# Last two feed-forwards multiply high and low input parts as one 512-column operand; recurrent gates take their Exp before their Ln

## The reference

```
def swiglu_2(u, w1, w3, w2):
    return (jax.nn.silu(u @ w1) * (u @ w3)) @ w2
```

## Time and profile before

| | |
|---|---|
| median of 3 runs | 2218.63 us (2211.37 to 2218.75) |
| profiled execution | 2217.61 us, of which the span is 2215.8 us |
| busy share of the span | TensorE 96%, its weight loads 86%, VectorE 72%, ScalarE 43% |
| L514, matmuls of all up steps | 7392, 903.3 us busy |
| L529, matmuls of the down steps | 1512, 355.0 us busy |
| L752, low parts of weights | 224, 512.5 us busy |
| L712, modulation rows (two groups) | 240, 294.3 us busy |
| granted TensorE clock, mean | 0.98 of full speed |

### The profile page before, as it was taken

The page is one execution under the profiler, slowest core; times in us unless marked ns, Lnnn a source line. Parts: engine busy times, 40 slices in busy tenths (PEclk is TensorE's granted clock), DMA queues, the critical chain, the costliest instruction groups (busy, mean ns, idle before and its releaser), DMA issues. The chain is left out here.

```text
span 2215.8 us, 37819 instructions
## 1 busy us (share of the span) xinstructions
PE 2125.2 (96%) x16108; PEld 1901.7 (86%) x16108; DVE 1596.1 (72%) x2307; ACT 959.2 (43%) x1330; POOL 2.3 (0%) x8
## 2 busy tenths in 40 slices
PE   7999999999999999999999899999899999999998
PEld 5999899887899999977999689888699996759997
DVE  4887877766787888766887678486677776666545
ACT  3444534426544353435434476343453444225333
POOL 0000000000000000000000000000000000000000
PEclk7999999999999999999999899999999999999999
DMA  9866588440688778733987112400278822305551
GB/s 395 329 245 259 219 318 337 156 153 3 231 353 322 292 285 322 312 143 121 368 322 299 46 58 83 154 15 3 79 278 349 346 91 84 152 1 198 196 185 38
DMA packets 65814, 450.86 MB, mean 203 GB/s; under 512 B 7959, under 2 KB 9240, under 8 KB 12696
## 3 DMA queue, kind: packets, MB, share of 16 engines
q1 hardware_dynamic: 65688, 449.11, 52.6%
HBM read 448.03 MB, written 1.05 MB: 203 GB/s over the span
## 5 line engine op out<-in xcount | busy, mean ns | idle before, releaser
L514 PEld LDWEIGHTS banks<-ffn_h_split,ffn_weights_split 128*128 128x128 f32 x7392 | 898.8, 192 | 13.3 <-DVE ffn_weights_split L589 4.7
L514 PE MATMUL banks<-ffn_h_split,ffn_weights_split 128*128 128x256 f32 x7392 | 903.3, 284 | 6.6 <-DVE ffn_h_split L610 6.3
L752 DVE TENSOR_TENSOR ffn_weights_split<-weight_ring,ffn_weights_split 128x2048 fp32r<-128x2048 f32 x224 | 512.5, 2288 | 236.8 <-ACT ffn_weights_split L656 236.8
L656 ACT CAST ffn_weights_split<-weight_ring 128x2048 fp32r<-128x2048 f32 x224 | 426.2, 1903 | 172.7 <-PE banks L529 165.0
L529 PE MATMUL banks<-ffn_weights_split,ffn_hidden_split 128*128 128x512 f32 x1512 | 355.0, 390 | 1.8 <-DVE ffn_hidden_split L689 1.8
L529 PEld LDWEIGHTS banks<-ffn_weights_split,ffn_hidden_split 128*128 128x128 f32 x1512 | 279.8, 188 | 57.6 <-DVE ffn_hidden_split L689 2.2
L624 ACT ACTIVATE ffn_arena<-banks 128x256 f32<-128x256 f32 x154 | 59.1, 384 | 504.5 <-PE banks L514 504.5
L712 DVE CUSTOM_DVE_ANT_0 weight_ring<-weight_ring,first_arena,cols 128x1024 f32<-128x1024 f32 x200 | 245.3, 1279 | 0.4 <-ACT first_arena L666 0.4
L696 DVE TENSOR_TENSOR ffn_arena<-banks,ffn_arena 128x256 f32<-128x256 f32 x154 | 64.8, 421 | 46.5 <-ACT ffn_arena L624 46.4
L539 PE MATMUL banks<-ffn_weights_split,ffn_hidden_split 128*128 128x512 f32 x336 | 77.6, 390 | 0.0
L539 PEld LDWEIGHTS banks<-ffn_weights_split,ffn_hidden_split 128*128 128x128 f32 x336 | 62.6, 188 | 12.7
(11 more groups left out here) (399 smaller groups left out, 2486.7 us busy)
## 6 DMA issues: line engine op xcount, KB each, us to landing
weight_ring<-in_weights SPq DMA_DIRECT2D x407, 1024.0 KB, 4.9
first_arena<-in_norm_rows SPq DMA_DIRECT2D x12, 512.0 KB, 7.1
first_arena<-in_c_rows SPq DMA_DIRECT2D x4, 512.0 KB, 11.6
first_arena<-in_ctx_rows SPq DMA_DIRECT2D x2, 1024.0 KB
h<-in_ctx SPq DMA_DIRECT2D x1, 1024.0 KB, 17.6
side<-in_x SPq DMA_DIRECT2D x1, 1024.0 KB
x<-in_x_rows SPq DMA_DIRECT2D x1, 1024.0 KB
hyena_tables<-in_hy_filt SPq DMA_DIRECT2D x1, 1024.0 KB
```

What stands on the lines that cost most here:

```text
L514: last = nc.tensor.matmul(bank[:, half * T:half * T + T], w[:, x, sl], hs[:, k, y, :], start=(k == 0 and x + y == 0), stop=(k == DT - 1 an ...
L656: nc.scalar.copy(wsplit[:, c % S, 0, :], raw).then_inc(self.split_hi.sem, 1)
L752: nc.vector.tensor_tensor(wsplit[:, c % S, 1, :], core.wbuf[:, (self.first + at(c)) % NSLOT, :], wsplit[:, c % S, 0, :].bitcast(F32), ALU. ...
```

## The change

In feed-forwards A and B (`wide=True`) the high and low parts of the input, which lie side by side, are the one moving operand of a 512-column matmul with the high weights; the product with the low weights stays a matmul of 256 columns, added onto the first half. A half of a tile now fills a whole bank, so a tile takes two banks and the four banks hold two tiles. The two 256-column halves of a bank must be added: ScalarE copies the second halves of both banks to SBUF (`copy_low`), VectorE adds the first halves to them (`add`), and only then follow Silu and the gate product. The order of the steps in the loop over c is changed too: copy, hidden_hi, Silu, weights on ScalarE; add, hidden_lo, gate, weights on VectorE.

In the recurrent stage the four Exp come first and the four Ln together after them; an evacuation of PSUM lies between. The high and low parts of chunk lv0 are made before the gates' loop instead of after it, and those of lv1 move up to about where lv0's were.

```diff
+        def up_wide(p, par, c, place, r=0, opening=False):
+            for t in range(2):
...
+                if not (opening and p == 0):
+                    pe.wait_ge(self.summed.sem, p * 2 + (self.summed.base + t - 1))
+                w = wsplit[:, (c + t) % S, :, :]
+                for half in range(2):
+                    bank = core.ps[4 + 2 * t + half]
+                    for k in range(DT):
...
+                        nc.tensor.matmul(bank[:, :], w[:, 0, sl], hs[:, k, :, :].rearrange("p y t -> p (y t)"),
+                                         start=(k == 0), stop=(k == DT - 1), skip_group_check=True)
+                        last = nc.tensor.matmul(bank[:, 0:T], w[:, 1, sl], hs[:, k, 0, :], start=False, stop=(k == DT - 1),
+                                                skip_group_check=True)
+                last.then_inc(self.multiplied.sem, 1)
...
+        def copy_low(q):
+            act.wait_ge(multiplied.sem, multiplied.base + chunk_of_tile(q) + 1)
+            if q >= 2:
+                act.wait_ge(self.gated.sem, self.gated.base + q - 1)
+            at = 4 + 2 * (q % 2)
+            nc.scalar.copy(f["sums"][:, q % 2, :, :], core.banks[:, at:at + 2, T:2 * T]).then_inc(self.copied.sem, 1)
+
         def silu(q):
...
+            if self.wide:
+                act.wait_ge(self.summed.sem, self.summed.base + q + 1)
+                raw = f["sums"][:, q % 2, 1, :]
...
         for c in range(1, 3 * PAIRS):
             q = TILE_OF.get(c - S)
+            if q is not None and self.wide:
+                copy_low(q)
+            if waiting is not None and self.wide:
+                hidden_hi(waiting)
             if q is not None:
                 silu(q)
-            if waiting is not None:
+            if waiting is not None and not self.wide:
                 hidden_hi(waiting)
...
+        def add(q):
+            dve.wait_ge(self.copied.sem, self.copied.base + q + 1)
+            at = 4 + 2 * (q % 2)
+            nc.vector.tensor_tensor(f["sums"][:, q % 2, :, :], core.banks[:, at:at + 2, 0:T], f["sums"][:, q % 2, :, :],
+                                    ALU.add).then_inc(self.summed.sem, 1)
...
             q = TILE_OF.get(c - S)
+            if q is not None and self.wide:
+                add(q)
+            if waiting is not None and self.wide:
+                hidden_lo(waiting)
             if q is not None:
                 gate(q)
...
             step(nc.scalar.activation(b["ea"][:, :], b["a_log"][:, :], ACT.Exp))
+            high("lv0")
             for i in range(4):
                 act.wait_ge(steps.sem, steps.base + 6 + 3 * i + 2)
                 step(nc.scalar.activation(lt[:, i, :], lt[:, i, :], ACT.Exp))
-                step(nc.scalar.activation(lt[:, i, :], lt[:, i, :], ACT.Ln, bias=core.one[:, 0:1]))
             act.wait_ge(padded.sem, padded.base + 1)
             half_out("gk00", raw_pair(0, 0))
+            for i in range(4):
+                step(nc.scalar.activation(lt[:, i, :], lt[:, i, :], ACT.Ln, bias=core.one[:, 0:1]))
             last_out("gk01", "gk0", raw_pair(0, 1))
-            high("lv0")
+            high("lv1")
...
-            high("lv1")
...
+            low("lv0")
             for i in range(4):
-                dve.wait_ge(exps.sem, exps.base + 3 + 2 * (i + 1))
+                dve.wait_ge(exps.sem, exps.base + 7 + i + 1)
...
-            low("lv0")
+            low("lv1")
             products(0), products(1)
...
-            low("lv1")
```

More of the change, by code:

```diff
@@ L457, in __init__ @@
     def __init__(self, core, h, f, tail, sides=None, refresh=None, modulate=None, vector=None, before=None,
-                 opening=None, split_next=False, ahead=()):
-        self.opening, self.split_next, self.ahead = opening, split_next, ahead
+                 opening=None, split_next=False, ahead=(), wide=False):
+        self.wide, self.opening, self.split_next, self.ahead = wide, opening, split_next, ahead
         self.core, self.h, self.f, self.tail, self.sides, self.refresh = core, h, f, tail, sides, refresh
@@ L469, in __init__ @@
         self.hid_hi, self.hid_ready = take("ffn_hidden_hi", FFT), take("ffn_hidden_ready", FFT)
+        self.copied, self.summed = take("attn_exp", FFT if wide else 0), take("attn_p_ready", FFT if wide else 0)
         self.modulated = take("ffn_modulated", DT + 1 if modulate else 0)
@@ L492, in pe @@
         assert all(at(c + 6 * r) == at(c) + body * r for c in range(5, 11) for r in range(rounds))
+        def up_wide(p, par, c, place, r=0, opening=False):
+            for t in range(2):
+                if opening and p == 0 and t == 0:
+                    pe.wait_ge(self.first_lo.sem, self.first_lo.base + 1)
+                else:
+                    pe.wait_ge(used.sem, r * body + (first + place[t] + 1))
+                if not (opening and p == 0):
[4 more added lines that the diff above has]
+                    for k in range(DT):
+                        if opening and p == 0 and t == 0 and half == 0:
+                            pe.wait_ge(self.h_lo.sem, self.h_lo.base + max(k, 1) + 1)
+                        sl = slice(k * 2 * P + half * P, k * 2 * P + half * P + P)
+                        nc.tensor.matmul(bank[:, :], w[:, 0, sl], hs[:, k, :, :].rearrange("p y t -> p (y t)"),
[3 more added lines that the diff above has]
+                last.then_inc(self.multiplied.sem, 1)
         def up(p, par, c, place, r=0, opening=False):
+            if self.wide:
+                return up_wide(p, par, c, place, r, opening)
             for t in range(2):
@@ L668, in act @@
             hidden_hi(waiting)
+        if self.wide:
+            copy_low(FFT - 1)
         silu(FFT - 1), hidden_hi(FFT - 1)
@@ L695, in gate @@
                 dve.wait_ge(self.hid_ready.sem, self.hid_ready.base + q - 1)
-            nc.vector.tensor_tensor(mul[:, q % 2, :], core.ps[4 + q % 4][:, 0:T], sg[:, q % 2, :], ALU.mult)\
+            nc.vector.tensor_tensor(mul[:, q % 2, :], value, sg[:, q % 2, :], ALU.mult)\
                 .then_inc(self.gated.sem, 1)
@@ L767, in dve @@
             hidden_lo(waiting)
+        if self.wide:
+            add(FFT - 1)
         gate(FFT - 1), hidden_lo(FFT - 1)
@@ L3226, in program @@
                             rows=[broadcast(12)], store=out, spread=1)
-                run(core, project, FeedForward(core, hf, f, tail, before=project))
+                f["sums"] = carve(2, 2, T)
+                run(core, project, FeedForward(core, hf, f, tail, before=project, wide=True))
 def _features(v):
```

11 lines of the change are left out of this document (8 added, 3 removed).

## The result

| us | before | after |
|---|---|---|
| median of the runs | 2218.69 (2211.37 to 2219.46, 8 runs) | 2226.10 (2223.14 to 2228.89, 8 runs) |
| profiled execution | 2217.61 | 2223.14 |
| span, mean granted clock | 2215.8, 0.980 | 2221.4, 0.985 |

The ratio is 1.0037, interval 1.0028 to 1.0046: slower by 8.2 us (6.2 to 10.2), which is within the 0.5% that the prediction calls "same". The predicted 2223.4 met the profiled execution, but the median lies 2.7 us higher; the part on why the prediction was right takes up both.

A forecast was written before the change was run, and what follows sets the result against it. TensorE bounds both feed-forwards before; after the change a VectorE-ScalarE chain bounds A. Terms: A +12.2, its half clock +1.6, B -3.7, recurrent stage -4.3, together +5.8 us on 2217.61, so 2223.4 us; range 2213 to 2230.

The forecast's parts named there:

- Ping-pong in A: Feed-forward A: VectorE and ScalarE bound the stage in turns, 17.67 us a period against TensorE's 16.60; A +12.2 us.
- half clock: A's end: after 6.5 us idle, TensorE runs at half clock, losing 1.6 us (bounds 0 and 3.2).
- TensorE's saving: Feed-forward matmuls: 11.9 ns less for each k and half, 4.2 us per feed-forward; B -3.7 us after its end.
- B's end: End of feed-forward B: tile 21's addition waits behind chunk 32's low part; 0.5 us given back.
- Recurrent stage: Recurrent stage: lv0 ready without a wait, last decay rows end earlier, -4.3 us (bounds -7.5 and -1.8).
- new wait: Recurrent stage: TensorE waits some 2.6 us before the third step of the decay rows.
- loads: Recurrent stage: six table loads of 1.28 us go on ScalarE, worth nothing there, even -0.5 us.
- what follows shifts with them: Behind the last decay rows: work dense on both engines moves earlier by the same 4.3 us.
- The sum: Whole kernel: +12.2 + 1.6 - 3.7 - 4.3 = +5.8 us on the profiled 2217.61, giving 2223.4 us.
- plain saving: Rival: A's chain is hidden and A gains 3.7 us as B does; -11.7, 2205.9 us; chance 0.08.
- The clock follows the gaps: Rival: A's 1.07 us idle per period each brings 3.2 us at half clock; +6.4, 2229.8 us; chance 0.09.

The follow-up runs named there:

- e1: Changed kernel with A's addition on VectorE moved between the two side chunks' modulation rows instead of behind both: 2211.3 us, ratio 0.9968.
- e5: Changed kernel with ScalarE making the weights' high part before Silu in A's steps that follow modulation rows: 2210.96 us, ratio 0.9975.
- e10: Changed kernel with each half tile's matmuls grouped by width, eight of 512 columns then eight of 256, addition left in place: 2226.56 us, ratio 1.0035.
- e3: Kernel before with only the recurrent part of the change, both feed-forwards narrow: 2215.66 us, ratio 0.9979.
- e6: Kernel before with only four Exp, evacuation, four Ln in place of the alternation; lv0's and lv1's parts not moved: 2214.77 us.
- e11: Changed kernel run a second time with no edit: 2226.21 us, ratio 1.0043 against the kernel before.

## Why the prediction was right

- **Ping-pong in A**, predicted 17.67 us a period, measured 17.70, and cut by e1 and e5 at two links. The last rows, the 6.18 us of idle time (6.5 predicted) and 1.7 us of half clock (1.6) followed. A came to +14.46 us, predicted 12.2 + 1.6 = 13.8. The last 36 matmuls start 192.17 us behind A's first up matmul, where the prediction has 1800.3 - 1608.66 = 191.64: that is 0.5 of the 0.66. TensorE's wait in a period was 0.85 us and not 1.07, since its own work took longer than forecast; the chain's length does not depend on that.
- **TensorE's saving** is the mis-sized term: "I take the value that the two pure streams give", 11.9 ns. In B, in turns, they save 3 x 119.9 - 353 = 7 ns; B gained 2.17 us up to its end steps, not 4.2, and 187.78 - 186.44 = 1.3 us in all instead of 3.7. The step that failed is the assumption of one price for the mixed stream: the same order also ran at 347 ns, the value taken, behind most waits in A (e10). What decides between the two prices stays open, so that the cause of this miss is known only as far as that. The Trainium skill, page "TensorE: Matmul & The Clock Gate", section "Back-to-back issue gap", leads to an estimate of 2.5 ns; the trace shows 7 and 13 ns, so that is too low, and by it B would have gained 0.4 us.
- **B's end** gave back 0.8 us; predicted 0.5, measured wait 0.52.
- **Recurrent stage**: no wait at lv0, new wait 2.5 us (2.6), product-sums from 1294.59 to 1300.54 (1294.7 to 1300.7), loads worth -0.56 (-0.5). The third decay job gained 4.17 us, predicted 4.3. At A's start 3.62 were left: "what follows shifts with them" did not quite hold, with 1.6 us of half clock in the way (e3). Behind the new wait TensorE's clock stayed at 1.00.
- **The sum**: by stages +14.46 - 1.34 - 3.62 = +9.5 us; predicted +5.8. Of the missing 3.7 B makes 2.4 (2.0 of it the matmuls), A and the recurrent stage 0.7 each. That the profiled execution came out at +5.5 is not of the prediction's making: 3.7 us fell away in and behind the Hyena stage (last section). The medians, 7.4 us apart (8.2 by the ratio), are nearer to the stages' sum. Every part had the right sign, and the range held the median, but the nearness of the single figure 2223.4 is luck.
- Of the rivals, "plain saving" fell, but e1 shows how near it was: one operation's place. "The clock follows the gaps" fell: with 0.85 us of idle time per period the clock in A stayed at 1.00.

## What to carry over

When an operation is put between a matmul and its evacuation, look at which engine makes it and what stands in that engine's queue ahead of it: here 4.8 us of unrelated rows turned two engines with idle time into the stage's bound. Spare time on both engines says nothing about a chain that passes between them; add up the chain once round the loop, and place the new operation where its inputs are ready, in the middle of the long work. Table loads saved off the path are worth nothing (e6).

## What the runs showed of the hardware

**Half clock behind the same wait, or not.** The opening of the Hyena stage in the kernel before: the idle time and the 4 us behind it; then the projection ahead of B. Below them the same three stretches of the changed kernel:

```profile
1802.00:1803.80 1.80, 0.00 (x0) 0.02 (x1) 1.49 (x4) 1.31 (x4) 0.00 (x0) 1.00 0.00 0
1803.80:1807.80 4.00, 3.99 (x21) 4.00 (x22) 3.68 (x11) 4.00 (x9) 0.00 (x0) 0.57 0.01 4
1984.40:1988.90 4.50, 4.45 (x7) 1.92 (x8) 2.92 (x6) 4.48 (x10) 0.00 (x0) 0.62 0.00 0
```

```profile
1812.40:1814.30 1.90, 0.01 (x2) 0.04 (x1) 1.57 (x4) 1.41 (x5) 0.00 (x0) 1.00 0.00 0
1814.30:1818.30 4.00, 4.00 (x35) 4.00 (x36) 3.69 (x11) 4.00 (x9) 0.00 (x0) 1.00 0.01 2
1992.80:1997.30 4.50, 4.42 (x11) 2.06 (x12) 2.90 (x6) 4.45 (x10) 0.00 (x0) 1.00 0.02 5
```

The waits are equal (1.90 and 2.15 us), the work is equal, the clock is not. Each such stretch costs 1.7 us. Of 13 profiles, 4 show the half clock behind the 1.90 us wait, 9 behind one of 1.6 us some 40 us later, 5 behind the 2.15 us one; the profile of the changed kernel had none of the three, the kernel before two. Between A's end and B's start this and small differences make the 2.4 and 1.3 us seen above, and so the profiled difference of 5.5 us where the stages give 9.5. Whether such a stretch comes by chance or goes with the program was not settled, with one profile for most kernels. Medians of the same kernel repeat better than such steps would suggest: 2217.7 to 2218.7 us in four sets for the kernel before, 2226.10 and 2226.21 for the changed one.

**Widths in turns have two prices.** A 512- and a 256-column matmul in turns cost 353 ns in B's periods and 347 ns in other tiles of the same profile, both at a granted clock of 1.00; in groups of eight 11.14 / 32 = 348. In A of the changed kernel the pair's second tile took 5.55 us (347 ns) behind seven of the nine waits and 5.65 or 5.66 behind two. In the second profile of that kernel (e11) five of nine were fast. In e1, with no such waits, the two tiles of the second pair, ahead of the first down step, were fast in A and in B, and all tiles behind it slow. In B of the changed kernel these two were slow as well; B's code is the same, and it takes 174.54 us to its end steps instead of e1's 174.23. So neither the order nor a wait of itself sets the price, and it stays open what does. The first matmul behind a wait costs 0.1 us more than the others (0.33 us to the next start instead of 0.23).
